# Gate and up products of the feed-forward steps with the weights stationary

## The reference, cut to what matters

```python
h2 = rms_norm(x, ffn_norm_g[l])
x = x + (jax.nn.silu(h2 @ w_gate[l]) * (h2 @ w_up[l])) @ w_down[l]
```

## Time and profile before

| what | value |
|---|---|
| median of 3 executions (lowest, highest) | 1249.5 us (1249.44, 1251.26) |
| the profiled execution, its own time | 1251.52 us |
| its span, first to last instruction | 1249.8 us |
| PE busy | 1228.5 us, 98% |
| PEld busy | 1037.9 us, 83% |
| DVE busy | 814.7 us, 65% |
| ACT busy | 664.4 us, 53% |
| DMA | 212.73 MB, mean 170 GB/s |
| granted clock of TensorE, mean | 0.997 of full speed |

### The profile page before, as it was taken

How to read it: one execution, slowest core, us unless ns; L and a number is a source line. 1 busy time by engine, 2 the same in 40 slices (tenths; PEclk the granted TensorE clock), 3 DMA queues, 4 the chain that set the end, 5 groups by cost and what they waited for, 6 DMA issues and landing times.

```text
span 1249.8 us, 16857 instructions
## 1 busy us (share of the span) xinstructions
PE 1228.5 (98%) x6398; PEld 1037.9 (83%) x6398; DVE 814.7 (65%) x979; ACT 664.4 (53%) x983; POOL 196.5 (16%) x174
## 2 busy tenths in 40 slices
PE   8999999999999999999999999999999999999998
PEld 6778888888887888888888899888997788888886
DVE  5899655545669966545447756876685697655544
ACT  5667454444555765443436355655547745644443
POOL 5885100001178730000000000000000030000000
PEclk9999999999999999999999999999999999999999
DMA  7523454556362254655545464343334455555551
GB/s 267 189 87 141 149 218 174 200 182 216 124 228 99 100 186 142 228 185 184 199 172 186 169 236 170 137 152 122 114 120 165 172 185 186 201 200 177 192 210 43
DMA packets 32795, 212.73 MB, mean 170 GB/s; under 512 B 3777, under 2 KB 3905, under 8 KB 10082
## 3 DMA queue, kind: packets, MB, share of 16 engines
q1 hardware_dynamic: 32674, 211.82, 47.5%
q0 software_dynamic: 64, 0.13, 0.0%
HBM read 210.88 MB, written 1.05 MB: 170 GB/s over the span
## 4 chain that ended last, share of the span: by engine, by line
PE 85%; DVE 6%; ACT 4%; POOL 2%; DMA 2%; issue 1%; SPq 0%; DVEq 0%; ACTq 0%; POOLq 0%
PE bank L599 25%; PE bank L601 25%; PE bank L600 25%; PE bank L1048 2%; DVE wlo L1765 2%; ACT probs L1367 2%; ACT whi L1290 1%; PE bank L883 1%; PE bank L629 1%; PE bank L794 1%; DMA raw<-in_w_out 1%; DVE z L2250 1%; PE bank L754 1%; PE bank L728 1%; POOL gain L518 1%
## 5 line engine op out<-in xcount | busy, mean ns | idle before, releaser
L1765 DVE TENSOR_TENSOR wlo<-raw,whi 128x2048 fp32r<-128x2048 f32 (+4 forms) x197 | 445.0, 2263 | 241.5 <-ACT whi L1290 239.5
L1290 ACT ACTIVATE whi<-raw 128x2048 fp32r<-128x2048 f32 (+5 forms) x201 | 369.3, 1842 | 131.5 <-PE bank L601 123.2
L599 PE MATMUL bank<-whi,hT_hi 128*128 128x512 f32 (+4 forms) x1028 | 401.6, 391 | 1.1 <-DVE wlo L1765 1.0
L601 PE MATMUL bank<-whi,hT_lo 128*128 128x512 f32 (+4 forms) x1028 | 392.5, 382 | 0.0
L600 PE MATMUL bank<-wlo,hT_hi 128*128 128x512 f32 (+4 forms) x1028 | 392.2, 382 | 0.0
L599 PEld LDWEIGHTS bank<-whi,hT_hi 128*128 128x128 f32 x1028 | 193.8, 189 | 38.6 <-issue 2.7
L601 PEld LDWEIGHTS bank<-whi,hT_lo 128*128 128x128 f32 x1028 | 193.4, 188 | 35.8
L600 PEld LDWEIGHTS bank<-wlo,hT_hi 128*128 128x128 f32 x1028 | 194.0, 189 | 32.6
L599 PE MATMUL bank<-whi,mixT_hi 128*128 128x512 f32 (+1 forms) x248 | 95.4, 384 | 0.2 <-DVE wlo L1765 0.2
L599 PE MATMUL bank<-whi,ffT_hi 128*128 128x512 f32 x240 | 93.7, 390 | 0.0
L601 PE MATMUL bank<-whi,ffT_lo 128*128 128x512 f32 x240 | 93.5, 390 | 0.0
(11 more groups left out here) (288 smaller groups left out, 1453.0 us busy)
## 6 DMA issues: line engine op xcount, KB each, us to landing
raw<-in_ff_loop SPq DMA_DIRECT2D x90, 1024.0 KB, 4.8
raw<-in_w_groups SPq DMA_DIRECT2D x64, 1024.0 KB, 4.7
raw<-in_w_out SPq DMA_DIRECT2D x8, 1024.0 KB, 5.6
raw<-in_ff_first SPq DMA_DIRECT2D x6, 1024.0 KB, 4.8
raw<-in_w_values SPq DMA_DIRECT2D x8, 728.0 KB, 4.1
raw<-in_w_comp SPq DMA_DIRECT2D x4, 1024.0 KB, 6.4
raw<-in_ff_last SPq DMA_DIRECT2D x3, 1024.0 KB, 4.7
raw<-in_w_values SPq DMA_DIRECT2D x4, 736.0 KB, 5.4
```

The costliest lines, as they stand in the source:

```text
L599: eng.matmul(out, lhsT=hi, rhs=wh, start=start, stop=False)
L601: return eng.matmul(out, lhsT=lo, rhs=wh, start=False, stop=stop)
L1290: eng.activation(whi[j][:, 0:n], raw[j][:, 0:n], ACT.Copy).then_inc(hi_ready, 1)
L1765: eng.tensor_tensor(wlo[j][:, 0:n], raw[j][:, 0:n], whi[j][:, 0:n].bitcast(F32), ALU.subtract).then_inc(lo_ready, 1)
```

## The change

Steps 1 to 10 of each layer change, step 0 keeps its products.

- The gate and up products are turned round. 128 columns of the weights are stationary (four blocks b: two of gate, two of up, in banks 0, 1, 6, 7). For `whi`, `hT_hi` and `hT_lo` move together as one operand of 2 x 256 columns, 8 KB apart in the partition, into the whole bank; for `wlo`, `hT_hi` alone, 256 columns, into the bank's first half. The result is already transposed: hidden columns on the partitions, 256 tokens in a row, as the sum of the bank's two halves.
- Per step 4 x 8 x 2 = 64 matmuls (32 of 512 columns, 32 of 256) take the place of 48 of 512.
- DVE adds the halves of each block (`tensor_reduce`, 512 to 256), multiplies gate by the tokens' norm factors, laid out along the row in `ff_rs` (two more transposes and one ACT copy per layer), and multiplies up by the silu of gate. ACT's silu reads SBUF. The norm factor of up is left out and put on the output of `down` instead: L2050 and L2038 become `scalar_tensor_tensor`, and the square gets a scale.
- `turn(c)` is gone for c from 1 on. `gate_up(c)` waits once, at its start, for all four sums of step c - 1 (`gu_free`).
- `turn(0)` writes banks 2 and 3 and has two more transposes behind it, into bank 4.
- ACT writes `ffT_hi` in one copy of 512 columns after `down(c - 1)` has ended; DVE `ffT_lo` in one.

```diff
-        hT = [sb(f"hT_{s}", [P, KT, SEQ], F32R) for s in ("hi", "lo")]
+        hT_both = sb("hT_both", [P, 2, KT, SEQ], F32R)
+        hT = [hT_both[:, s] for s in range(2)]
...
+        ff_raw = probsT[:, 0:2, 0:FF_STEP]
+        ff_gate = probsT[:, 0:2, FF_STEP:2 * FF_STEP]
+        ff_up = headsT[:, 0:2, :]
+        ff_prod = headsT[:, 2:4, :]
+        ff_rs = headsT[:, 4, :]
+        ff_bank = (0, 1, 6, 7)
...
+                def block_half(b, k0, i):
+
+                    wh, wl = whi[i % RING], wlo[i % RING]
+                    for k in range(k0, k0 + 4):
+                        w = slice((k - k0) * UNIT + b * P, (k - k0) * UNIT + (b + 1) * P)
+                        eng.matmul(bank[ff_bank[b]][:, :], lhsT=wh[:, w], rhs=hT_both[:, :, k, :],
+                                   start=(k == 0), stop=False)
+                        mm = eng.matmul(bank[ff_bank[b]][:, 0:SEQ], lhsT=wl[:, w], rhs=hT_both[:, 0, k, :],
+                                        start=False, stop=(k == 7))
+                    return mm
+
+                def gate_up(c):
+
+                    i = i0 - 1
+                    eng.wait_ge(lo_ready, done_at(t0 + c, i))
+                    if isinstance(c, int) and c == 1:
+                        for r in range(RT):
+                            bank_read(r)
                     else:
+                        eng.wait_ge(gu_free, blocks_freed(l, c))
+                    for b in range(4):
+                        mm = block_half(b, 0, i)
+                    mm.then_inc(used, 1)
+                    if isinstance(c, int) and c == 1:
+                        turn_first()
+                    eng.wait_ge(lo_ready, done_at(t0 + c, i + 1))
+                    for b in range(4):
+                        block_half(b, 4, i + 1).then_inc(used if b == 3 else gu_ready, 1)
...
+                def turn_first():
                     for r in range(RT):
-                        eng.wait_ge(gu_free, l * 2 * FF_STEPS + 2 * c + 1 + r)
+                        eng.wait_ge(gu_free, rows_freed(l) + 1 + r)
                         for k in range(2):
-                            mm = eng.transpose(bank[6 + r][:, k * P:(k + 1) * P],
+                            mm = eng.transpose(bank[2 + r][:, k * P:(k + 1) * P],
                                                probs[:, r, k * P:(k + 1) * P], ident[:, :])
                         mm.then_inc(ff_turned, 1)
+                    for r in range(RT):
+                        mm = eng.transpose(bank[4][:, r * P:(r + 1) * P],
+                                           ssq[:, 4 + r:5 + r].to_broadcast([P, P]), ident[:, :])
+                    mm.then_inc(ff_rs_turned, 1)
 
                 three.act = hT
-                gate_up(0)
+                first_rows()
                 gate_up(1)
                 down(0, i0 + 4, True)
-                turn(1)
-                with eng.Fori(2, FF_STEPS - 1) as c:
+                with eng.Fori(2, FF_STEPS) as c:
                     gate_up(c)
                     down(c - 1, i0 + 4, False)
-                    turn(c)
-                last = FF_STEPS - 1
-                gate_up(last)
-
-                down(last - 1, i0 + 4, False, between=lambda: turn(last))
-                last_down(last, i0 + 2)
+                last_down(FF_STEPS - 1, i0 + 2)
 
...
+                    eng.wait_ge(ff_rs_turned, l + 1)
+                    eng.activation(ff_rs, bank[4][:, 0:SEQ], ACT.Copy).then_inc(ff_rs_ready, 1)
+                    split_hi(t0, i + 5)
+                def step(c, last=False):
+                    i, done = i0 - 1, pairs_done(l, c)
+                    split_hi(t0 + c, i + 3)
+                    for b in range(2):
+                        eng.wait_ge(ff_scaled, done + b + 1)
+                        eng.activation(ff_gate[:, b, :], ff_raw[:, b, :], ACT.Silu).then_inc(silu_ready, 1)
+                    if last:
+                        if more:
+                            split_hi(t0 + c, i + 4, 2 * UNIT)
+                        for b in range(2):
+                            eng.wait_ge(ff_ready, done + b + 1)
+                            eng.activation(mixT[0][:, b, :], ff_prod[:, b, :], ACT.Copy).then_inc(ff_hi, 1)
+                        if more:
+                            split_hi(t0 + c, i + 5, 2 * UNIT)
+                        return
+                    split_hi(t0 + c, i + 4)
+                    eng.wait_ge(ff_ready, done + 2)
+                    eng.wait_ge(used, done_at(t0 + c - 1, i0 + 4))
+                    eng.activation(ffT[0][:, :, :], ff_prod, ACT.Copy).then_inc(ff_hi, 2)
+                    split_hi(t0 + c, i + 5)
+                first_rows()
...
+                def halves_sum(b, out):
+                    eng.tensor_reduce(out, bank[ff_bank[b]][:, :].rearrange("p (s c) -> p c s", s=2), AX.X,
+                                      ALU.add).then_inc(gu_free, 1)
+                def step(c, last=False):
+                    i, done = i0 - 1, pairs_done(l, c)
+                    ready = l * (1 + 3 * (FF_STEPS - 1)) + 1 + 3 * (c - 1)
                     split_lo(t0 + c, i + 3)
+                    for b in range(2):
+                        eng.wait_ge(gu_ready, ready + b + 1)
+                        halves_sum(b, ff_raw[:, b, :])
+                        eng.wait_ge(gu_free, blocks_freed(l, c) + b + 1)
+                        eng.tensor_tensor(ff_raw[:, b, :], ff_raw[:, b, :], ff_rs, ALU.mult).then_inc(ff_scaled, 1)
+                    for b in range(2):
+                        if b == 0:
+                            eng.wait_ge(gu_ready, ready + 3)
+                        else:
+                            eng.wait_ge(used, done_at(t0 + c, i + 1))
+                        halves_sum(2 + b, ff_up[:, b, :])
+                        eng.wait_ge(gu_free, blocks_freed(l, c) + 3 + b)
+                        eng.wait_ge(silu_ready, l * 2 * FF_STEPS + 2 * c + b + 1)
+                        eng.tensor_tensor(ff_prod[:, b, :], ff_up[:, b, :], ff_gate[:, b, :], ALU.mult)\
+                           .then_inc(ff_ready, 1)
+                    hi_count = l * 2 * FF_STEPS + 2 * c
+                    if last:
+                        for b in range(2):
+                            eng.wait_ge(ff_hi, hi_count + b + 1)
+                            eng.tensor_tensor(mixT[1][:, b, :], ff_prod[:, b, :], mixT[0][:, b, :].bitcast(F32),
+                                              ALU.subtract).then_inc(ff_lo, 1)
+                        if following is not None:
+                            split_lo(t0 + c, i + 4, 2 * UNIT)
+                            split_lo(t0 + c, i + 5, 2 * UNIT)
+                        return
+                    split_lo(t0 + c, i + 4)
+                    eng.wait_ge(ff_hi, hi_count + 2)
+                    eng.tensor_tensor(ffT[1][:, :, :], ff_prod, ffT[0][:, :, :].bitcast(F32), ALU.subtract)\
+                       .then_inc(ff_lo, 2)
+                    split_lo(t0 + c, i + 5)
+                first_rows()
+                eng.wait_ge(ff_rs_ready, l + 1)
...
-                        eng.tensor_tensor(part, part, bank[2 + 2 * n + r][:, :], ALU.add).then_inc(down_added, 1)
+                        eng.scalar_tensor_tensor(out=part, in0=bank[2 + 2 * n + r][:, :], scalar=ssq[:, 4 + r:5 + r],
+                                                 in1=part, op0=ALU.mult, op1=ALU.add).then_inc(down_added, 1)
```

More of the change, by code:

```diff
@@ L798, in ffn, with first_rows @@
             def ffn(t0, i0, l, norm, bank_read, following=None):
[L799 to L804, removed]
+                def first_rows():
+                    out = bank[4:6]
                     def tile(r, k0, i, turn_at=0):
@@ L844, in gate_up @@
[L844 to L848, removed]
+                    tile(0, 0, i0)
+                    turn_half(norm, 1)
+                    tile(1, 0, i0).then_inc(used, 1)
+                    eng.wait_ge(turned_lo, norm * 4 + 4)
+                    eng.wait_ge(lo_ready, done_at(t0, i0 + 1))
+                    tile(0, 4, i0 + 1).then_inc(gu_ready, 1)
@@ L850, in down @@
+                def down(c, i, first):
                     eng.wait_ge(ff_lo, l * 2 * FF_STEPS + 2 * c + 2)
                     eng.wait_ge(lo_ready, done_at(t0 + c, i))
+                    if first:
+                        eng.wait_ge(ff_rs_ready, l + 1)
                     three.act = ffT
                     for kk in range(2):
-                        if between and kk == 1:
-                            between()
                         for n in range(2):
@@ L1398, in ffn, with first_rows @@
             def ffn(t0, i0, l, norm, stats, more):
-                def step(c, out=bank, first=False, last=False):
-                    dst = mixT if last else ffT
-                    i = i0 - 1
-                    split_hi(t0 + c, i + 3)
-                    early = first and l == LAYERS
-                    if first:
-                        stats()
-                        if early:
```

(35 more changed lines are left out.)

99 lines of the change are left out of this document (32 added, 67 removed).

## The result

| | before | changed |
|---|---|---|
| median of 22 executions each (lowest, highest) | 1250.49 us (1249.11, 1251.46) | 1252.27 us (1250.90, 1254.19) |
| the profiled execution, its time and span | 1251.52, 1249.8 us | 1253.67, 1251.8 us |

The ratio is 1.0017 with a 95% interval of 1.001 to 1.0023: slower, by about what a measurement of this kernel can tell. The prediction had 1243.8 us, faster, and its range of 1239 to 1249 does not hold the result. Ten turns a layer are gone, and nothing came of it.

A forecast was written before the change was run, and what follows sets the result against it. The kernel was taken to last as long as PE's stream of matmuls. The terms 6.4 - 14.1 + 0.66 + 1.2 + 0.1 gave -5.7 us, from a median of 1249.5 to 1243.8 us; range 1239 to 1249.

The forecast's parts named there:

- Products turned: Gate and up products per step: 10.89 us becomes 11.10, +0.21; +6.4 us over 10 steps of 3 layers.
- rival 1: A 256-column matmul between two of 512 pays no fixed part; the +6.4 falls away: 1237 to 1238 us; chance 0.12.
- The turn: 30 turns (steps 1 to 10, three layers) of 0.47 us each go from PE: -14.1 us.
- The moving operand in two runs: High and low rows 8 KB apart in the 512-column matmuls: taken as nothing, upper bound 12.8 us in all.
- Rival 2: Operand in two runs costs a second fixed part, 0.0133 us in 960 matmuls: 12.8 us slower, 1256.6 us; chance 0.07.
- DVE's sums: In the loop, 0.69 us per sum; the fourth done at 14.1 to 14.8, PE asks at 16.54: no cost.
- rival 3: DVE's sums take 1.38 us each, so PE waits in the steps: +23 us, 1266 us; chance 0.05.
- Step 1: Thin cover for DVE's fourth sum: PE waits 0.4 us in each layer, +1.2 us.
- Step 10: `last_down` needs the split of the products at 16.54, ready at 15.4 to 16.2: no cost.
- rival 4: Small waits in step 1 and step 10 add 1.3 us a layer, +3.9 us: 1247.7 us; chance 0.12.

## Why the prediction was wrong

The step that failed is *Products turned*: "48 x 0.2268 = 10.89 becomes 32 x 0.2268 + 32 x 0.1200 = 11.10". Both prices are right, and each was measured only among its own kind. The alternating stream took 0.3533 a pair in the loop, 6.5 ns more than their sum. So the products of a loop step took 11.29 and not 11.10, and the slow matmuls at `down`'s start brought it to 5.50 and not 5.44: 16.79 and not 16.54. Over the three layers the trace shows 7.1 us of this (30 steps at the loop's price would be 7.6, but the second half of each step 1 was in the faster rhythm), which is more than the 5.7 that were forecast as gain. The prediction noted under rival 1 that this sequence is not in the trace, and used that for a gain only; the bound on the other side was not drawn, so no rival had this price.

Point by point for the rest:

- *The turn*, 0.47: right in the old stream; 0.41 ahead of a mixed one in the slower rhythm.
- *The moving operand in two runs*: nothing, as taken. Rival 2 had the right sign for a wrong reason, and its time, 1256.6, was 4 us too high.
- *Extra matmuls cheaper* (rival 1): wrong; a 256-column matmul pays its full 13 ns in every arrangement run.
- *DVE's sums*, 0.69: 0.68. The Trainium skill (VectorE: DVE Perf Modes, Rules for kernel authors) calls `tensor_reduce` the slowest operation; here it was no longer than an addition of as many elements (0.68 in the earlier trace rows), and rival 3 had no ground. The timeline of DVE in the loop step:

```profile
237.07 2.29 DVE L1815 TENSOR_TENSOR wlo<-raw,whi 128x2048 fp32r<-128x2048 f32 x1 [2.77 <-ACT whi L1326]
239.28 0.68 DVE L2058 TENSOR_REDUCE probsT<-bank 128x256 f32<-128x512 f32 x1
239.99 0.42 DVE L2070 TENSOR_TENSOR probsT<-probsT,headsT 128x256 f32<-128x256 f32 x1
...
242.56 0.68 DVE L2058 TENSOR_REDUCE headsT<-bank 128x256 f32<-128x512 f32 x1
243.36 0.42 DVE L2079 TENSOR_TENSOR headsT<-headsT,probsT 128x256 f32<-128x256 f32 x1
```

  The fourth sum is done at 243.24, 13.97 into the step (forecast 14.1 to 14.8), and PE asks 2.8 us later: hidden, as said.
- *Step 1*: the fourth sum was done at 178.76, as reckoned, but the weight load stood idle for only 0.2 a layer and the stream lost 0.06 (287 ns and not 227 behind the first matmul of the loop), where 0.4 was taken: 1.0 us less than in the sum. *Step 10*: no wait, as said; rival 4 did not come.
- *Outside the change*: +1.4 us by the fetch of instructions. The prediction counted what moves on each queue and not that PE's own code moves.

The differences add up as 7.1 + 1.4 - 1.0 = 7.5 us. By the medians of 22 the change costs 1.8 us where 5.7 of gain were forecast, and that is 7.5 too; single profiles differ by 1 us in the first 100 us alone, so the last tenths are no proof. The forecast of 1243.8 missed by 8.5 us, because it stood on a median of 3 executions that is 1 us below that of the 22.

What is shown: the size of the slower rhythm, that the operand's form is not its cause, that grouping by length avoids it, and that the faster rhythm exists for the very same order. What stays open: the mechanism inside PE, and what exactly brings one rhythm or the other behind a break in the stream. For the fetch, it is shown that the packet's place decides; not why 16 KB delay a load of 1 MB by over 1 us.

## What to carry to other kernels

A price per matmul that is read from a stream of equal ones holds for such a stream; where lengths alternate, read the price from an alternating stream or group the matmuls by length, which cost nothing here and was worth 0.22 to 0.24 us in 16.8. Where an effect is below some 0.2% of the time, look whether the code's length has moved a fetch of instructions into a load, before it is put down to the change; padding at one place near it tells, padding at the kernel's start moves all the others too.

## What the runs showed that was not expected

- Two rhythms of one instruction stream: three pairs in 1060 ns or in 1040, in consecutive iterations of one loop, with the clock granted in full.
- A matmul of 16, 20, 24 or 28 columns between two of 512 takes 0.118 us of the stream, whatever its length. The Trainium skill (TensorE: Matmul & The Clock Gate, LDWEIGHTS) puts the load of 128 weight columns at about 107 ns, which such a matmul is too short to hide; an estimate from it and the 13 ns of the earlier trace rows is 120, and by that rule the trace agrees in what the stream pays. The records of single weight loads do not: they are 188 ns long.
- A load of 1 MB takes 6.0 to 6.6 us from issue to use where a packet of 16 KB of PE's instructions starts 1.2 to 3.1 us into it, and 4.8 to 5.0 where the packet starts 4.4 us into it or 2.4 before it.
